# Two-block transformer stack on one Trainium2 core: step inputs with weights held, gated recurrence with decays built by products

## The reference, cut to what matters

```python
dt = jax.nn.softplus(dt_raw.reshape(b, L, 2, SSM_HEADS) + dt_bias)
```

```python
ff = lb + (1.0 - lb) * jax.nn.sigmoid(f)      # log_f = log(ff), k = 1 - ff
# S_t = diag(f_t) S_{t-1} + k_t v_t^T,  o_t = S_t^T q_t
decay = jnp.exp(jnp.where(mask, diff, -jnp.inf))          # diff = cum_t - cum_s
scores = jnp.einsum('bhtsk,bhsk->bhts', q_c[:, :, :, None, :] * decay, k_c)
```

## Time and profile before

| | us |
|---|---|
| median of 3 runs | 3496.81 |
| the profiled execution, its time | 3497.71 |
| its span (first to last instruction) | 3496.4 |
| TensorE busy | 3355.9 (96%), 21944 products |
| VectorE busy | 2065.5 (59%) |
| ScalarE busy | 1337.2 (38%) |
| GpSimd busy | 82.7 (2%), 60 instructions |

### The profile page before, as it was taken

The page is one execution under the profiler, slowest core; times in us unless marked ns, Lnnn a source line. Parts: engine busy times, 40 slices in busy tenths (PEclk is TensorE's granted clock), DMA queues, the critical chain, the costliest instruction groups (busy, mean ns, idle before and its releaser), DMA issues.

```text
span 3496.4 us, 53221 instructions
## 1 busy us (share of the span) xinstructions
PE 3355.9 (96%) x21944; PEld 2741.4 (78%) x21944; DVE 2065.5 (59%) x3837; ACT 1337.2 (38%) x2480; POOL 82.7 (2%) x60
## 2 busy tenths in 40 slices
PE   7989999999999999999999999999999989999998
PEld 6777788888888778788888888667677677788887
DVE  6776753554447776744644457765666589664334
ACT  4456543332224566543332323222443234232222
POOL 0000000000000000000000000000000044000000
PEclk9999999999999999999999998999999999999999
DMA  4221223233334221223333333323311324333332
GB/s 134 83 68 49 56 78 107 91 99 97 97 99 129 78 74 44 57 76 115 97 97 97 97 106 89 91 76 111 119 31 34 112 73 151 100 114 98 98 97 85
DMA packets 353816, 314.73 MB, mean 90 GB/s; under 512 B 11348, under 2 KB 281812, under 8 KB 353576
## 3 DMA queue, kind: packets, MB, share of 16 engines
q1 hardware_dynamic: 352712, 309.10, 29.4%
q10 hardware_dynamic: 864, 2.23, 0.2%
HBM read 287.69 MB, written 23.59 MB: 89 GB/s over the span
## 4 chain that ended last, share of the span: by engine, by line
PE 80%; DVE 13%; ACT 4%; issue 3%; DMA 1%; POOL 0%; DVEq 0%; SPq 0%; ACTq 0%; POOLq 0%
PE banks L528 13%; PE banks L530 13%; PE banks L529 13%; PE banks L427 9%; PE banks L429 8%; PE banks L428 8%; DVE weights_r L368 2%; PE banks L628 1%; PE banks L2678 1%; PE banks L2617 1%; PE banks L1100 1%; PE banks L1113 1%; PE banks L1204 1%; ACT weights_high_r L361 1%; PE banks L2375 1%
## 5 line engine op out<-in xcount | busy, mean ns | idle before, releaser
L368 DVE TENSOR_TENSOR weights_r<-weights,weights_high_r 128x1024 fp32r<-128x1024 f32 (+3 forms) x520 | 598.7, 1159 | 347.4 <-ACT weights_high_r L361 346.5
L528 PE MATMUL banks<-h_T_hi,weights_high_r 128*128 128x512 f32 (+2 forms) x1904 | 759.2, 399 | 12.8 <-DVE cellsB L3665 5.1
L530 PE MATMUL banks<-h_T_hi,weights_r 128*128 128x512 f32 (+2 forms) x1904 | 736.1, 387 | 0.0
L529 PE MATMUL banks<-h_T_lo,weights_high_r 128*128 128x512 f32 (+2 forms) x1904 | 735.5, 386 | 0.0
L361 ACT ACTIVATE weights_high_r<-weights 128x1024 fp32r<-128x1024 f32 (+3 forms) x520 | 510.7, 992 | 360.8 <-DMA weights<-in_w_mlp 212.8
L528 PEld LDWEIGHTS banks<-h_T_hi,weights_high_r 128*128 128x128 f32 x1904 | 360.7, 189 | 104.0 <-issue 30.2
L530 PEld LDWEIGHTS banks<-h_T_hi,weights_r 128*128 128x128 f32 x1904 | 360.2, 189 | 72.9
L529 PEld LDWEIGHTS banks<-h_T_lo,weights_high_r 128*128 128x128 f32 x1904 | 361.1, 190 | 69.2 <-issue 3.6
L427 PE MATMUL banks<-weights_high_r,h_T_hi 128*128 128x512 f32 (+3 forms) x704 | 290.8, 413 | 11.3 <-ACT cellsX L577 6.0
L429 PE MATMUL banks<-weights_high_r,h_T_lo 128*128 128x512 f32 (+3 forms) x704 | 267.1, 379 | 0.0
L428 PE MATMUL banks<-weights_r,h_T_hi 128*128 128x512 f32 (+3 forms) x704 | 266.5, 379 | 0.0
(11 more groups left out here) (567 smaller groups left out, 5357.9 us busy)
## 6 DMA issues: line engine op xcount, KB each, us to landing
weights<-in_w_in SPq DMA_DIRECT2D x182, 512.0 KB, 3.8
weights<-in_w_mlp SPq DMA_DIRECT2D x128, 512.0 KB, 3.7
weights<-in_ffn_w_in SPq DMA_DIRECT2D x44, 512.0 KB, 3.8
weights<-in_w_out SPq DMA_DIRECT2D x24, 512.0 KB, 3.6
weights<-in_ffn_w_down SPq DMA_DIRECT2D x22, 512.0 KB, 3.6
weights<-in_w_mem_kv SPq DMA_DIRECT2D x16, 512.0 KB, 3.6
weights<-in_w_diff_o SPq DMA_DIRECT2D x16, 512.0 KB, 3.5
weights<-in_w_mla_o SPq DMA_DIRECT2D x8, 512.0 KB, 3.4
```

Of the source, the lines that this page charges most:

```text
L368: ve.e.tensor_tensor(self.part(c.w_raw_r, u), self.part(c.w_raw, u), self.part(c.w_high_r, u).bitcast(F32), ALU.subtract).then_inc(*ve.tel ...
L528: pe.e.matmul(out, lhsT=wh[:, k, :], rhs=hi[k][:, cols], start=(k == 0), stop=False)
L529: pe.e.matmul(out, lhsT=wh[:, k, :], rhs=lo[k][:, cols], start=False, stop=False)
L530: mm = pe.e.matmul(out, lhsT=wl[:, k, :], rhs=hi[k][:, cols], start=False, stop=(k == self.chunks - 1))
```

## The change

Step inputs: the job of `Tokens` becomes one unit of `Features` over 128 columns of the weights (32 of them are wanted, the other 96 products are not used). ScalarE copies the 32 rows out, TensorE turns them into tokens (four transposes) and VectorE adds the bias. The plan's later times move with it.

Recurrence: logarithms, running sums, exponents and GpSimd's part are gone. Keys and queries are kept with their decays inside the current piece, and each level multiplies half of them by the total decay of the neighbouring piece (`double`); totals of joined pieces are products (`total`). The products of a level read the queries of both directions alternately piece by piece (`crossed`), and ScalarE copies the keys together in the same way. After the last level the same arrays serve the scan.

Constants: TensorE no longer waits for the small vectors, and the two mask transfers stand one step later in SyncE's program.

```diff
@@ Constants2
         sp.e.dma_start(self.vectors, c.i["vectors_2"]).then_inc(*sp.tell("vectors2_in", by=16))
+        yield
         sp.e.dma_start(self.small_masks, c.i["masks_small"]).then_inc(*sp.tell("masks_in", by=16))
...
-        self.c.pe.wait_ge("vectors2_in")
@@ StateSpace and its new helpers
+class DtRows(Sink):
+    def act(self, f, key, got):
+        ac.e.activation(self.rows, got[0:2 * SH, :], ACT.Copy).then_inc(*ac.frees(*key))
+class DtTurn(Stage):
+    def pe(self):
+        pe.wait_all(self.rows_in)
+        bank = c.fill("dt turn")
+        for t in range(NT):
+            mm = pe.e.transpose(bank[:, t * 2 * SH:(t + 1) * 2 * SH], self.rows[:, t * P:(t + 1) * P], c.ident[0:2 * SH, 0:2 * SH])
...
-        self.dt_job = Tokens(c, "dt", c.hT, KD, w[:, C_DT:C_RW], DtOut(c, lambda t: self.four(self.dt)[:, t, :], k.dt_bias, free), ring="gemm 2", together=2,
-                             tile_ready=norm.done)
+        self.dt_job = Features(c, "dt", c.hT, KD, w[:, C_DT:C_DT + P], DtRows(c, rows, free), ready=norm.done(), ring="gemm 2")
@@ Block2, plan
-        plan.at(k, (0.6, 3.1, 14))
+        plan.at(k, (0.6, 3.1, 18.2))
-        plan.beside(Steps(ssm), 30, 42)
+        plan.at(ssm.dt_turn, (ssm.conv.jobs[0].n + ssm.dt_job.n + 1.5,))
+        plan.beside(Steps(ssm), 18, 30)
@@ GatedRecurrence, scores
-    def scores_pool(self):
...
-                gp.e.tensor_tensor(k4[:, :, d, :], ends[d], cu[d][:, :, d, :], ALU.subtract).then_inc(*gp.step())
...
+            ac.wait_ge("level_scaled", n)
...
+            ac.e.activation(self.X[:, heads, :].rearrange("p h s -> p (h s)"),
+                            self.crossed(self.keys_all, heads.start * S, 2 * S, 1 << lev), ACT.Copy).then_inc(*ac.tell("level_keys", n))
...
-                ve.e.tensor_tensor_scan(w, self.mask, w, 0.0, ALU.mult, ALU.add).then_inc(*ve.tell("cumulated", d, h))
...
+        def double(n):
...
             for d in range(2):
+                keys, queries = k4[d][:, :, d, :], q4[d][:, :, 1 - d, :]
+                ve.e.tensor_tensor(keys, keys, (second, first)[d][d], ALU.mult).then_inc(*ve.step())
+                ve.e.tensor_tensor(queries, queries, (first, second)[d][d],
...
+        def total(n):
...
+                ve.e.tensor_tensor(last, last, totals[:, :, :, 0, at], ALU.mult).then_inc(*ve.tell("totals", n))
...
+        for n in range(self.scored + 1):
+            double(n)
+            if n:
+                keep(n - 1)
+            total(n)
+            if n == self.scored:
+                double(n + 1)
+                total(n + 1)
+                ve.settle()
+            yield
@@ GatedRecurrence, scan
-        ac.e.activation(u["X"], self.cum[d], ACT.Exp).then_inc(*ac.tell("scan_decay", d))
...
-                ve.e.tensor_tensor(w, w, self.key[d][:, :, tok], ALU.mult).then_inc(*ve.tell("end_keys", d, n))
```

More of the change, by code:

```diff
@@ L3281, in cut, with crossed @@
         return x.rearrange("p h s -> p (h s)").rearrange("p (n a b) -> p n a b", a=2, b=size)
[L3283 to L3287, removed]
+    def crossed(self, x, at, cols, size):
+        return bass.AP(x.tensor, x.offset + at, [list(x.ap[0]), [2 * size, cols // (2 * size)], [size + HH * S, 2], [1, size]])
     def level_products(self, n):
-        c, pe, (_, _, _, keys, queries) = self.c, self.c.pe, self.level(n)
+        c, pe, (lev, heads) = self.c, self.c.pe, self.levels[n]
+        size = 1 << lev
         for j in range(NT // 2):
@@ L3307, in scores_pe @@
         yield
-        for n in range(len(self.levels)):
-            pe.wait_ge("level_scaled", n)
+        for n in range(self.scored):
+            pe.wait_ge("level_keys", n)
             self.level_products(n)
@@ L3374, in scores_dve, with ends @@
         yield
[L3376 to L3380 removed]
+        def ends(n):
+            lev, heads = self.levels[n]
+            return self.total_all[:, :, heads, :].rearrange("p d h s -> p d (h s)").rearrange("p d (n a b) -> p d n a b", a=2, b=1 << lev - 1)
+        def double(n):
+            lev, heads = self.levels[n]
+            if lev == 0:
+                for d in range(2):
+                    ve.e.tensor_tensor(self.asked[d][:, heads, :], self.q[:, heads, :], self.total[d][:, heads, :],
+                                       ALU.mult).then_inc(*(ve.tell("level_scaled", n) if d else ve.step()))
+                return
+            half, totals = 1 << lev - 1, ends(n)
+            wide = lambda x: x.broadcast_to([P, S // half, half])
+            k4, q4 = ([self.cut(x[:, heads, :], half) for x in y] for y in (self.key, self.asked))
+            first, second = ([wide(totals[:, d, :, a, half - 1:half]) for d in range(2)] for a in range(2))
+            ve.wait_ge("filled", "level", n - 2, NT // 2 - 1)
+            ve.wait_ge("level_scaled", n - 2)
+            if lev > 1:
+                ve.wait_ge("totals", n - 2)
             for d in range(2):
[L3382 to L3383 removed]
+                keys, queries = k4[d][:, :, d, :], q4[d][:, :, 1 - d, :]
+                ve.e.tensor_tensor(keys, keys, (second, first)[d][d], ALU.mult).then_inc(*ve.step())
+                ve.e.tensor_tensor(queries, queries, (first, second)[d][d],
                                    ALU.mult).then_inc(*(ve.tell("level_scaled", n) if d else ve.step()))
+        def total(n):
+            lev, heads = self.levels[n]
+            if lev:
+                totals, at = ends(n), (1 << lev - 1) - 1
+                last = totals[:, :, :, 1, at]
+                ve.wait_ge("level_scaled", n)
+                ve.e.tensor_tensor(last, last, totals[:, :, :, 0, at], ALU.mult).then_inc(*ve.tell("totals", n))
         def keep(n):
@@ L3418, in scan_pe @@
             if d == 0:
-                pe.wait_ge("emptied", "level", len(self.levels) - 1, t // 2)
+                pe.wait_ge("emptied", "level", self.scored - 1, t // 2)
             if d == 0 or n:
```

163 lines of the change are left out of this document (59 added, 104 removed).

## The result

| | us | ratio to before, 95% interval |
|---|---|---|
| before, median of 4 runs | 3497.22 | |
| after, median of 4 runs (3458.63 to 3472.76) | 3470.27 | 0.9913 [0.9888, 0.9938] |
| after once more, 5 runs (3466.12 to 3473.14); before 3496.11 | 3468.93 | 0.9921 [0.9907, 0.9934] |

The forecast was 3468.7, in a range of 3457 to 3483. The profiled execution was the shortest of all, 3458.63 us. In the record of the granted clock its stretches at half clock add up to 60.3 us, against 101.7 in the one before; half of that, 30.2 against 50.9, is lost time.

A forecast was written before the change was run, and what follows sets the result against it. TensorE, busy 96% of the span, was taken as the bound. Step inputs 14.5 plus levels 13.6 gave 28.1 us off the profiled 3497.71, 3469.6; that execution lay 0.9 above the median, so 3468.7, range 3457 to 3483.

The forecast's parts named there:

- Bound: Whole kernel: TensorE busy 96% of the span, so only its waits, lower clock or removable work count.
- Step inputs, 14.5 us: Second block's step inputs: 19.06 removed + 2.4 clock − 5.44 new products − 0.5 transposes − 1.0 lateness = 14.5 us.
- a late arrival of the vectors: Step inputs: larger weight splits and small vectors queued behind bigger transfers cost 1.0 us, with 0 and 3 as ends.
- second rival: Step inputs: clock falls as before and small vectors come late, 2.4 + 2.4 + 2 us less gain; 3475.5 us; 13%.
- Constants count zero: Small vectors and masks: dropping TensorE's wait and moving the mask transfers one step changes nothing, zero us.
- Levels: Recurrence's levels: 17.0 us of waits and 3.8 of slow clock go, new costs 3, 1.5 and 2.7; gain 13.6 us.
- Alternating read: Levels' products: TensorE reading queries alternately from two places costs 1.5 us, between 0 and 27.
- third rival: Levels: each of 112 products at 0.12 us takes three times as long, using up the gain; four times, 3508 us; 3%.
- Single words: VectorE's doublings from 1 to 2 tokens and two totals: 5 to 9 us more, sum up to 5 us worse.
- Turn, 2.7 us: End of the levels: two doublings and a total ahead of L656 make TensorE wait 2.7 us more.
- First rival: Levels: VectorE stays the bound, doublings costing 1.4 us for a reason other than GpSimd; 3484 us; 12%.

The follow-up runs named there:

- the busy GpSimd: Changed kernel with GpSimd put back to work in the levels, 16 subtractions of 128 elements on an unread constant beside each level; one execution, 3483.34 us.
- repeated profile: The changed kernel run once more with no edit, profiled for its usual execution; median 3468.93 us, profiled execution 3469.07 us.

## Why the prediction was right, point by point

- **Bound.** Right: TensorE's time is what counted. Taking out GpSimd's work alone, which TensorE never waits for directly, gave 16.5 us through TensorE's waits.
- **Step inputs, 14.5 us.** Right in its products (5.50 us for 24, 5.44 said) and in the turn (0.43, 0.5 said). The sum is 14.8 to 15.4 us in the five profiles where the clock stayed, and 7.2 and 7.4 in the two where the last tile came 2.2 us late; alone it measured 11.8. The term that was mis-sized is "a late arrival of the vectors on top does not" fit, which I took at 1.0 with an end of 3: the wait itself grew by 0.5 or 1.6 us, within the ends, but in both executions with the longer wait the clock fell behind it, at a price that my 1.0 to 3 did not hold. That was the second rival (2.4 + 2.4 + 2 less), and it describes one execution of the usual kind; I gave it 13% as if it were all or nothing, where it comes and goes.
- **Constants count zero.** Right for the kernel before (1.0004), and the whole change has no wait of TensorE on the vectors. Not seen was that the new transfers ahead of the vectors would have made this wait dear: left in its place, it cost 2.0 us and a slow stretch. And the arithmetic on them, which the change left ahead of the last tile, is how the late vectors reached TensorE. I had looked at TensorE's wait on them and not at what ScalarE's wait (L1943) has queued behind it, the last tile's high part.
- **Levels.** Right in kind and size: 15.1 us alone, 13.6 said. VectorE was busy for 106 us (115 said), a doubling took 0.685 (0.645 said), and 17.0 us of waits became 2.6 (3 said). The Trainium skill (SBUF — State Buffer, "SBUF: two separate sides") gave VectorE's rate back once GpSimd was gone, and so it came: 1384 to 685 ns by that one edit. That the loser stands still for a whole instruction no run shows: the longest of the 28 keys' products took 1.77 us, less than 0.68 and one of GpSimd's 2.04 together. What I had not seen is how much hung on it. The fewer operations of the new scheme, which I worked out at length, added nothing that shows: without GpSimd the old scheme is as fast (16.5 us, 12 to 22 by its interval, against 15.1, 9 to 18), as far as these runs can tell.
- **Alternating read.** 0.97 + 0.87 + 0.13 + 0.14 = 2.1 us, 1.5 said, all in the pieces of one and two tokens; the third rival's three times did not occur, the worst is 1.5 times. That rival's arithmetic was off by two: a level has 16 products in the profile, so there are 224 at 0.12 us, not 112, and 28 us would have been used up at about twice the time.
- **Single words.** The Trainium skill (Vector Engine (DVE) Microarchitecture Reference, "5.2 Measured stream behaviour on trn2") spoke of 1.7 to 2.5 times for such streams. The doublings of the first level, words two apart, take 0.69 like all others: the trace does not agree. It comes near for the totals of the next level, where the words lie four apart: 1.08 for 512 against 0.685, 1.6 times, worth 0.8 us for the two of them on an engine with slack.
- **Turn, 2.7 us.** Right in kind, and the size partly by luck. I had put all of it down to TensorE's wait for L656. That wait grew by 0.7 us (4.4 to 5.1) in the first profile and by 2.1 in the repeated one; the rest of the 2.3 and 4.7 us lost goes with a longer stretch at half clock (10.2 and 13.7 us instead of 3.4), which was in no term.
- **First rival** (VectorE stays the bound): it fell with GpSimd, and the busy GpSimd shows a part of what it would have looked like: doublings of 0.85 us, but VectorE busy for 116.55 of 144 us.
- **The number is better than the account.** The repeated profile lies 28.6 us under the one before, as good as the 28.1 forecast. But its step inputs gave 7.4 us (14.5 said) and levels and turn 15.0 (13.6 said). The rest is in no term: 8.9 between the two places, 0.5 behind them, less 3.1 ahead of the block. Errors that cancel are luck. Of the 8.9, 3.4 go with less half clock and 4.0 with shorter stops in the delta rule, whose cause is open (end of this document).

## What to carry to other kernels

An engine with little work can hold up the one that feeds the bound: GpSimd was busy for 2% of the span, and leaving its work out gave 16.5 us. Try the kernel with such an engine's work left out before rewriting the work. A part that measures nothing alone can be needed by another part: TensorE's wait on the vectors was free until larger transfers stood ahead of them. In two profiles a wait of 2.2 us ahead of short products was followed by 13.7 us at half clock, so small vectors' arithmetic had better not stand in the queue in front of the tile that TensorE waits for. What only a later stage needs goes behind the turn that TensorE waits for, even where the engine looks idle on the average.

## What the runs showed of the hardware that I had not expected

- ScalarE's copy of 1024 elements took 1.53 to 1.56 us where it read single elements alternately from two places, 1.22 for pairs, 1.06 from four on; TensorE's 16 products 2.9, 2.1 and 1.95; VectorE's operations did not slow down at single elements two apart.
- VectorE's reads of PSUM (L3423, 734 ns in the mean with GpSimd silent, and 731 with GpSimd busy) were not slowed by GpSimd; its products of two operands in SBUF were.
- In the delta rule TensorE stands still at two small groups of products with no releaser. The five kernels of these runs that have the step inputs as 96 products lose 2.2 us or more there, the eight profiles with 24 products 0.4 to 1.2, though nothing near it was changed. The list of waits of the kernel before (2700 to 2762):

```profile
PE banks L2655 <- issue: 1.5, 1, 1.5
PE banks L2617 <- issue: 1.5, 1, 1.5
```

And of the changed kernel, the same place (2681 to 2741):

```profile
PE banks L2645 <- issue: 0.7, 1, 0.7
```

That the 72 products fewer ahead of it are the cause was not tried; what TensorE waits for there stays open.
